# One encoder step on one core: the first heads' bias loads, a block of output weights, scale rows, four dots and a gate moved to other places in the program

## What is computed

```python
sh1, sc1, g1, sh2, sc2, g2 = modulation(c, w_ada, b_ada)
h = rmsnorm(x, norm1_g) * (1 + sc1) + sh1
z = h @ w_in                                   # GLU value, GLU gate, q, k, v
y_conv = silu(layernorm(causal_dwconv(u)))     # u = za * sigmoid(zg), width 31
o = attn(q, k, v)                              # 16 heads of 64, learned relative bias
x = x + g1 * (concat(y_conv, o) @ w_out)
h2 = rmsnorm(x, norm2_g) * (1 + sc2) + sh2
# PEER: 8 heads, top 16 of 128 x 128 experts, one u row and one v row each
q = h2 @ w_pq ; scores against sub_keys ; top-k ; g = softmax
act = gelu(dot(h2, u_experts[picked]))         # 128 dots a row
x = x + g2 * sum((g * act) * v_experts[picked])
```

## Time and profile before

| | |
|---|---|
| median of 3 runs | 3911.17 us |
| lowest, highest | 3910.19, 3914.08 us |
| the profiled execution, its own time | 3912.98 us |
| its span in the trace | 3911.2 us |
| PE busy | 3659.4 us, 94% |
| DVE busy | 2665.0 us, 68% |
| moved by DMA | 1418.49 MB, mean 363 GB/s |

### The profile page before, as it was taken

The page is one execution under the profiler, slowest core; times in us unless marked ns, Lnnn a source line. Parts: engine busy times, 40 slices in busy tenths (PEclk is TensorE's granted clock), DMA queues, the critical chain, the costliest instruction groups (busy, mean ns, idle before and its releaser), DMA issues.

```text
span 3911.2 us, 34419 instructions
## 1 busy us (share of the span) xinstructions
PE 3659.4 (94%) x12521; PEld 1929.5 (49%) x12521; DVE 2665.0 (68%) x4253; ACT 444.2 (11%) x975; POOL 1022.0 (26%) x888
## 2 busy tenths in 40 slices
PE   5899999998998898899989999999998899999996
PEld 2566545476543663466734444444465344444443
DVE  1258853157888788878986777767688754555666
ACT  2100004110000440102600000000052000000000
POOL 1000001215324344343232222222233322222331
PEclk8999999998999799999999999999999999999998
DMA  9878773559999899999799999999989999999997
GB/s 387 274 247 275 256 290 128 198 204 405 413 414 417 331 379 413 395 406 361 266 415 421 414 411 422 421 419 418 417 294 358 421 421 380 421 422 422 421 417 310
DMA packets 337760, 1418.49 MB, mean 363 GB/s; under 512 B 26009, under 2 KB 134529, under 8 KB 195742
## 3 DMA queue, kind: packets, MB, share of 16 engines
q0 software_dynamic: 120752, 848.17, 53.8%
q1 hardware_dynamic: 215840, 563.29, 37.8%
q10 hardware_dynamic: 1008, 4.98, 0.3%
HBM read 1390.84 MB, written 47.28 MB: 368 GB/s over the span
## 4 chain that ended last, share of the span: by engine, by line
DMA 50%; PE 31%; issue 12%; DVE 5%; POOL 2%; ACT 1%; DVEq 0%; POOLq 0%; SPq 0%; ACTq 0%
DMA R<-in_u_experts,MS 36%; DMA R<-in_v_experts,MS 10%; PE bank L895 8%; PE bank L926 7%; PE bank L1119 4%; PE bank L1298 3%; DMA R<-in_w_ada 2%; DVE R L2321 2%; PE bank L840 1%; POOL R L776 1%; DVE R L2201 1%; PE bank L1294 1%; PE bank L812 1%; PE bank L1183 1%; DMA R<-in_w_in 1%
## 5 line engine op out<-in xcount | busy, mean ns | idle before, releaser
L776 POOL DMA_INDIRECT R<-in_u_experts,MS x640 | 817.9, 1278 | 1699.1 <-DVE MS L2201 1477.7
L2201 DVE CUSTOM_DVE_ANT_0 R<-R 128x2048 f32<-128x2048 f32 x374 | 856.6, 2291 | 383.3 <-DMA R<-in_u_experts,MS 361.8
L1328 PE MATMUL bank<-R,RB 128*128 128x512 f32 x2304 | 1024.6, 603 | 48.2 <-DMA R<-in_v_experts 48.2
L1328 PE MATMUL bank<-RB 128*128 128x512 f32 x1792 | 778.2, 592 | 0.0
L1328 PEld LDWEIGHTS bank<-R,RB 128*128 128x128 f32 x2304 | 443.1, 193 | 619.6 <-issue 559.1
L2201 DVE CUSTOM_DVE_ANT_0 R<-R,RB 128x2048 f32<-128x2048 f32 x266 | 608.6, 2288 | 124.2 <-DMA R<-in_u_experts,MS 123.4
L1328 PEld LDWEIGHTS bank<-RB 128*128 128x128 f32 x1792 | 340.5, 190 | 428.6 <-issue 428.6
L2321 DVE SCALAR_TENSOR_TENSOR R<-R,MS 128x2048 f32<-128x2048 f32 x128 | 301.5, 2355 | 198.1 <-DMA R<-in_v_experts,MS 197.7
L895 PE MATMUL bank<-RB,R 128*128 128x256 f32 (+1 forms) x1536 | 399.8, 421 | 23.2 <-DMA R<-in_w_pq 18.8
L895 PEld LDWEIGHTS bank<-RB,R 128*128 128x128 f32 x1536 | 294.0, 193 | 122.6 <-DMA R<-in_w_pq 19.3
L1119 PE MATMUL bank<-RB,R 128*128 128x384 f32 x1024 | 334.9, 487 | 10.1 <-DMA R<-in_w_in 8.8
(11 more groups left out here) (355 smaller groups left out, 2248.5 us busy)
## 6 DMA issues: line engine op xcount, KB each, us to landing
R<-in_v_experts SPq DMA_DIRECT2D x144, 1024.0 KB, 9.1
RB<-in_v_experts SPq DMA_DIRECT2D x112, 1024.0 KB, 9.1
R<-in_w_ada SPq DMA_DIRECT2D x48, 2048.0 KB, 14.0
R<-in_w_in SPq DMA_DIRECT2D x20, 2048.0 KB, 18.8
R<-in_w_in SPq DMA_DIRECT2D x24, 1024.0 KB, 33.4
R<-in_w_out SPq DMA_DIRECT2D x8, 2048.0 KB, 8.4
R<-in_w_pq SPq DMA_DIRECT2D x8, 2048.0 KB, 10.6
R<-in_w_out SPq DMA_DIRECT2D x16, 1024.0 KB, 33.0
```

The source lines that it names most:

```text
L776: pool.indirect_dma_start(dst, None, table, bass.IndirectOffsetOnAxis(ap=expert[T_ % 2][:, c:c + 1], axis=0)).then_inc(signal, 16)
L1328: x = pe.matmul(PB[4 * h + q][:, :], W[:, i, h * P:(h + 1) * P], vring[slot][:, q * PW:(q + 1) * PW], start=(i == 0), stop=(i == NKEY - 1))
L2201: V.tensor_tensor_reduce(u, u, x, 1.0, 0.0, ALU.mult, ALU.add, dots[t % 2][:, h * TOPK + s:h * TOPK + s + 1]).then_inc(dots_done, 1)
```

## The change

It touches five things.

- SP: the first block of `w_out` is no longer loaded between the two halves of the value stores, but behind the loads of head 3 (and their wait for the maximum of head 1).
- SP: the scale rows (`A2Y`, `n2Y`) are loaded behind the third block of `w_out` instead of the second, and the first `B2Y` behind the fourth instead of the third; DVE combines the scale rows at v = 7 instead of 4.
- DVE: 20 dots instead of 16 after the heads, and none at v = 9, 10 and 11.
- PE: 34 unused products instead of 22 at head 0, and 2 new ones at head 1.
- ACT: `gate_exp(1)` and `gelu(1)` ahead of the thirteenth group of the last key queries instead of behind all.

```diff
             values_out(0)
-            load_block(6, "w_out", 0)
             values_out(1)
...
                 if b == 1:
                     values(hp)
+                if h == 3:
+                    load_block(6, "w_out", 0)
...
             for b in range(7, 10):
                 load_block(b, "w_out", (b - 6) * PW)
-                if b == 7:
+                if b == 8:
                     spread(A2Y, 1, s_sc2)
                     sp.dma_start(n2Y, n2rows_d[:, :]).then_inc(s_n2, 16)
-                if b == 8:
+                if b == 9:
                     sp.wait_ge(s_A2, 3)
                     sp.dma_start(B2Y[0], modrows_d[2, 0]).then_inc(s_sh2, 16)
...
+                if h == 1:
+                    stay_busy(5, 2)
                 pe.wait_ge(mx_ready, NH + h)
...
                 if h == 0:
-                    stay_busy(5, 22)
+                    stay_busy(5, 34)
...
                 for n in range(16):
+                    if G and n == 12:
+                        gate_exp(1)
+                        gelu(1)
                     act.wait_ge(q_done, 16 * G + n + 1)
...
-            gate_exp(1)
-            gelu(1)
             copy_turned(0)
...
-            steps(16)
+            steps(20)
...
-                if v == 4:
+                if v == 7:
                     dve.wait_ge(s_sc2, 16 * 2)
...
                 elif v == 3 * TY:
-                    steps(2)
                     dve.wait_ge(s_A2, 3)
                     dve.wait_ge(s_sh2, 16)
                 elif v < 4 * TY:
                     norm_tile(TX + v - 3 * TY - 1, A2Y[0], B2Y[0])
-                    steps(1)
```

## The result

| | before | changed |
|---|---|---|
| median of 15 runs | 3911.17 us | 3928.39 us |
| lowest, highest | 3902.68, 3926.06 us | 3915.87, 3941.90 us |
| ratio to before | | 1.0035, 95% interval 1.0022 to 1.0049 |
| the profiled execution, its own time | 3912.98 us | 3936.04 us |

The changed kernel is slower by 0.35% by the ratio, some 14 us (the medians are 17 us apart). It was run in two more groups, each beside before: 1.0014 (0.9997 to 1.0031) and 1.0036 (1.0021 to 1.0050). Forecast was 3910, with a range of 3893 to 3923. The time lies outside it, on the side that the forecast gave 0.21. The profiled execution of the changed kernel is one of its slower ones, 7.65 us above its median, so not all that its trace shows is the change.

What follows compares the result with a forecast made beforehand. Neither PE nor DMA alone was taken as the bound; where DMA is full, a dot costs its gather. Head stage -6 and dots and norms +5 gave -1 us from 3911.17: 3910, range 3893 to 3923.

Steps and rivals of the forecast that it cites:

- Head 0: At head 0, DVE's 9.49 us wait for biasC goes; its maximum ends 12 us earlier, near 1281.
- The ten cheaper dots: Before head 0, with the block gone from DMA, some ten dots each 0.45 us cheaper: 4.5 us.
- The stall at head 4: At head 4, DVE newly waits about 11 us for the bias behind the moved block; bounds 0 and 20.
- Pace and clock: Heads 0 to 4 at 8.07 us each, 32.3 instead of 39.9; PE's rest at head 4 costs 2.5 us.
- Dots and norms: Tenth residual (T0) 12.9 us later, last norm at T0 + 26.5, 8.3 sooner after it; net +5 us.
- Block 3 and the scale rows: PE's 12.76 us wait at block 3 goes, up to 15 us appears at block 4; price 0, bounds -3 and +3.
- Gate values: Ahead of ACT's thirteenth keep, before the build: no effect, 0 us, bounds -1 and +1.
- C: Chance 0.19: block not let through at the heads, q1 at a fifth of the bytes; stall 20, +10 us, 3921.
- A: Chance 0.40: the wait goes from head 0 to head 4, as worked out; 3901 to 3917.
- B: Chance 0.29: the block is absorbed by free engines between 1290 and 1320; -15 us, 3896.
- D: Chance 0.09: the head stage's gain or loss is handed back further on, at latest at the build; 3911.
- E: Chance 0.03: the block passes at once, landing within 14.4 us of issue, before head 4's bias is wanted; -13 us, 3898.

Runs made afterwards that it cites:

- the first experiments: Each part of the change alone on the kernel before: block behind head 3 with products 1.0008, dots 1.0003, gate values 0.9998, scale rows 1.0008.

## Why the prediction was wrong, point by point

**What bounds the kernel** was right as far as it went. Not seen was that the argument "where DMA is full" holds for nearly everything behind 1440 as well, the norms and the build excepted, so that the sum could have been made in bytes.

**Head 0: right in kind, a third too large.** No wait for `biasC`, as forecast. Without the two traces that were late from the start (below), the maximum came at 1285.2, 1278.4, 1284.3 and 1280.6, mean 1282.1; the five with the block in its old place have 1290.0 on the mean. That is 8 us, where I had 12. (With the two it is 1285.8; counted from SP's last `in_w_in` issue, which takes the late start out, all six are at 106.5 us and the five at 114.2, again 8.) The ten cheaper dots (4.5 us) brought 3, by the end of the last dot. And PE was not kept busy: its products ended at 1269.4 instead of 1273.7 (in the third trace at 1262), it rested 10.23 us, and `L1186` took 3.78 us as before, which DVE waited for (3.77).

**The stall at head 4: the failed step.** Right was that it comes, where, and for which row. I gave it 11 us with bounds of 0 and 20; it is 17.5, and 16.0 to 17.3 in five other traces. The sum was 14.4 us for q1 and 18.2 for seven gathers, 32.6. Measured are 38.7 us from head 1's maximum: q1 took 49.5% of it, 19.2 us, and the gathers 52.2%, 20.2 us for 8.14 MB, 7.8 gathers. So the step that failed is the term for q1, 4.8 us too small, and behind it that for the gathers, 2.0. I had the block and 2.75 us for head 3, the average of ten heads. But 7.07 MB went through, 2.9 more than the block. Every second head has the cached keys and values of a pair on top, and head 3 is one: SP issued 1.7 MB for it between 1291.8 and 1295.3, where the average is 1.0 MB a head. That, the block and head 4's bias (0.3 MB) leave 0.8 MB, which fits the rows of head 5 only: they were sent behind the bias and moved in part before it had landed.

**Pace and clock.** The four heads that I priced at 8.07 us went faster (47.9 us less the wait of 17.5 is 7.6 each), but heads 4 to 15 took 92.3 us instead of 88.8 after the rest of 15 us: 3.5 where I had 2.5. The clock was 1.00 in 1290 to 1320, as forecast. With the parts: -8, then heads 0 to 4 in 47.9 instead of 39.9, then 3.5: +3.5 for the head stage, which agrees with the 2.8 by bytes. I had -6. Of the 9.5 between them the stall is 6.5, head 0 is 4 and the clock 1, and the quicker heads give 2 back.

**Dots and norms: right.** +12.9 for the tenth residual: with the dots moved, head 15 to it takes 209.9 to 215.0 us, without 198.6 to 201.3, on the means +13.0 (seven and eleven traces). Last norm at T0 + 26.5: measured 1667.6 - 1640.4 = 27.2. From the tenth residual to the queries it is 30.5 us on the mean with the dots moved and 38.7 without: 8.2 saved, against my 8.3. The store of x is what DVE now waits for, 3.18 us. My +5 is 4.7 by the durations and 6.4 by bytes. That the group with the dots alone (1.0003) does not show it by time is within its error.

**Block 3 and the scale rows: right.** The wait moved to the fourth block, 10.56 us, at no cost in the residuals' distance (200.3 us with the rows alone moved, 199.3 before).

**Gate values: right as far as the runs tell.** The first trace seemed to say otherwise. It has a read-back of key scores of 16.2 us on the chain of waits, before 9.6, and the same kernel later 11.0 (the chain: start, us, what; before, changed, changed a third time):

```profile
1838.55 9.62 DMA R<-RB
```
```profile
1848.20 16.16 DMA R<-RB
```
```profile
1846.26 10.98 DMA R<-RB
```

Over all 18 traces it is 8.7 to 11.9 us in seven of the eight with the gate values early, 16.2 in the eighth, and 9.6 to 12.8 in the ten without. My theory of the first experiments, that DVE's wait had kept DMA free for it, fell with these.

**The rivals.** The time came out nearest to C's 3921, and head 4's rows landed at 1331 (C's point was "after about 1332"), with a stall near its 20. That is partly luck, for C's mechanism did not come. It had q0 never empty and q1 at a fifth of the bytes throughout. The trace has that only while gathers are queued: from 1302 to 1314 there are 512 packets of q0 and 543 of q1, with 3.80 and 1.12 MB. DVE stands still from 1313.7 on, its gathers run out, and in 1326 to 1331 q1 moves 1.95 MB alone. In all six traces with the block behind head 3 the last gather's packet starts 5 to 7 us ahead of the bias. What came is A's mechanism, a finite number of gathers in the way, with more on q1 than A had. B fell with the stall. D, that a gain or loss is handed back at latest at the build, fell too: at 1960 us, when the build has begun, the bytes moved still go with the span. E fell as well: in the six traces head 4's bias landed 34 to 36 us behind the block's first issue, not 14.4.

The Trainium skill, "DMA: Bandwidth & Descriptors", section "Queues, rings and completion order", has an engine drain a whole packet of descriptors from one ring before it switches. The traces do not decide on it. Nearly equal counts, 512 and 543 here, 625 and 623 in the earlier trace rows, come out of turns of one row as well as of turns of ten, and either way the bytes go by the size of the rows. So E does not follow from the page: it needs longer turns on one queue than on the other.

**The range.** Its upper end of 3923 was C's price and one gather. The 8 to 9 us that durations and bytes give would have stayed within it, at about 3920; together with the scatter of a chip's group they do not. And 0.21 for the slower side was too little. I took the middle of the stall's bounds (0 to 20), though the earlier trace rows pointed to the upper end: at 1.24 MB in 14 us the block's 4.19 MB would take 47 us if gathers were queued all the time. What is left between these 8 to 9 us and the 14 of the first group stays open.

## What to carry to other kernels

Where a later stage is bound by transfers, count the bytes that have been moved at its start beside the waits ahead of it: an idle wait costs little if DMA is full meanwhile (PE rested 33.9 us at head 0 in the version with 22 products and the block behind head 1, the DMA share in 1210 to 1290 was 1.01, and the time was 0.9984 of before), and a tidy schedule is dear if it leaves DMA empty. A large load that shares a queue with small urgent ones belongs right behind an urgent one that needs no wait (here head 1's), or in pieces between several; both came out 0.2% below before here. Right in front of one it makes that one wait, here for 16 to 17.5 of the 34 to 36 us that it takes to pass. And compare events within one trace before two executions' times are compared.

## What the runs showed of the hardware

- Executions of one program differ before anything of the change is reached. By 1143 us before had moved 328.8 MB, and others 325 to 331. Of the two late traces of the head 3 versions, with SP's last `in_w_in` issue at 1191 instead of 1167 to 1178, one has, by 1143 us,

```profile
DMA packets 157462, 325.25 MB, mean 285 GB/s; under 512 B 5556, under 2 KB 106140, under 8 KB 140531
```

  Four of the 18 traces have 325.0 to 325.3 MB by then, the others 328.8 to 331.1. Those four executions took 9.5 to 13.1 us more than the median of their own group, the other fourteen lie within 7.7 us of theirs, and over all 18 the correlation is -0.90. So the start is most of the scatter among the profiled executions, and why a single one misleads. What makes it stays open.
- The same 16 cached-key products take 1.95 us at full and 3.78 us at half the granted clock. How long it stays low varies: with the same program up to there heads 0 to 4 took 38.7 to 39.9 us in four traces and 46.7 in a fifth, at a mean clock of 0.65 in 1290 to 1345.
- While gathers and block rows were both queued, q0 and q1 moved about as many packets each (512 and 543 in 12 us), so q1 with its 2 KB rows got a fifth of the bytes, 1.12 MB beside 3.80. Once no gather was queued it moved 1.95 MB in 5 us.
- One transfer of key scores beside the same gathers took 8.7 to 16.2 us.
